# A mixture-of-experts loop: where the transposes, the rows given back and the down products stand in TensorE's list

## What is computed

```python
logits = t @ router_w + router_b
top_val, top_idx = lax.top_k(logits, 4)          # 4 of 32 experts for each token
gates = jax.nn.softmax(top_val, axis=-1)
...
# for each expert, with xe the rows of its tokens
gu = xe @ w_gu[e] + b_gu[e]                      # 1024 -> 2048
g, u = jnp.split(gu, 2, axis=-1)
g = jnp.minimum(g, 7.0)
u = jnp.clip(u, -7.0, 7.0)
act = (u + 1.0) * (g * jax.nn.sigmoid(1.702 * g))
y = act @ w_down[e] + b_down[e]                  # 1024 -> 1024
...
# weighted by the gates, added to the tokens' rows; then the gated residual add and rms_norm
```

## Time and profile before

| | |
|---|---|
| median of 3 runs | 1328.81 us |
| the profiled execution, own time | 1330.05 us |
| its span, first to last instruction | 1328.3 us |
| TensorE products, busy | 1272.8 us (96%) |
| TensorE weight loads, busy | 587.8 us (44%) |
| VectorE busy | 516.7 us (39%) |
| ScalarE busy | 178.1 us (13%) |
| read from memory | 476.10 MB, 359 GB/s over the span |

### The profile page before, as it was taken

The page is one execution under the profiler, slowest core; times in us unless marked ns, Lnnn a source line. Parts: engine busy times, 40 slices in busy tenths (PEclk is TensorE's granted clock), DMA queues, the critical chain, the costliest instruction groups (busy, mean ns, idle before and its releaser), DMA issues.

```text
span 1328.3 us, 16731 instructions
## 1 busy us (share of the span) xinstructions
PE 1272.8 (96%) x5975; PEld 587.8 (44%) x5976; DVE 516.7 (39%) x1144; ACT 178.1 (13%) x378; POOL 12.5 (1%) x31
## 2 busy tenths in 40 slices
PE   6999999999999999999999999999999999899997
PEld 4876866788753333333333333333333333233332
DVE  3022674331244434344343333333344344334344
ACT  2101322331021001000010000001100011001002
POOL 0000000110000000000000000000000000000000
PEclk8999999999999999999999999999999999999999
DMA  9857675326678999999999999999999999799995
GB/s 354 306 205 265 244 250 194 127 82 272 235 284 336 428 429 429 428 429 429 428 428 429 428 428 429 428 429 428 412 428 429 430 427 429 321 429 429 429 427 208
DMA packets 59182, 477.53 MB, mean 360 GB/s; under 512 B 4991, under 2 KB 5076, under 8 KB 32532
## 3 DMA queue, kind: packets, MB, share of 16 engines
q1 hardware_dynamic: 58852, 476.11, 87.3%
q10 hardware_dynamic: 304, 1.06, 0.2%
HBM read 476.10 MB, written 1.05 MB: 359 GB/s over the span
## 4 chain that ended last, share of the span: by engine, by line
PE 77%; DMA 18%; DVE 3%; issue 1%; ACT 1%; DVEq 0%; ACTq 0%; SPq 0%
PE bank L1610 24%; DMA down_ring<-in_w_down 17%; PE bank L1647 15%; PE bank L1294 11%; PE bank L1438 4%; PE bank L1287 4%; PE bank L1598 3%; PE bank L1576 3%; PE bank L1342 2%; PE bank L1501 2%; PE bank L1568 2%; DVE scratch L1125 1%; DVE scratch L1123 1%; DMA xres<-in_x 1%; PE bank L1677 1%
## 5 line engine op out<-in xcount | busy, mean ns | idle before, releaser
L1610 PE MATMUL bank<-gu_ring,scratch 128*64 128x512 f32 x2048 | 459.3, 595 | 1.6 <-DVE scratch L1055 1.6
L1610 PEld LDWEIGHTS bank<-gu_ring,scratch 128*64 128x64 f32 x2048 | 143.3, 137 | 284.7 <-issue 284.4
L1647 PE MATMUL bank<-down_ring,scratch 128*64 128x512 f32 x1024 | 235.5, 602 | 23.2 <-DMA down_ring<-in_w_down 18.1
L1294 PE MATMUL bank<-gu_ring 128*128 128x256 f32 x640 | 143.8, 381 | 0.0
L1647 PEld LDWEIGHTS bank<-down_ring,scratch 128*64 128x64 f32 x1024 | 71.0, 137 | 145.6 <-issue 133.5
L1294 PEld LDWEIGHTS bank<-gu_ring 128*128 128x128 f32 x640 | 119.8, 190 | 20.3 <-issue 4.0
L715 ACT ACTIVATE scratch<-bank 128x512 f32<-128x512 f32 x32 | 19.1, 597 | 684.6 <-PE bank L1610 684.6
L1113 DVE TENSOR_TENSOR scratch<-bank,bgu 128x512 f32<-128x512 f32 x32 | 22.1, 691 | 219.5 <-PE bank L1576 219.5
L1081 DVE TENSOR_TENSOR xres<-xres,bank 128x512 f32<-128x512 f32 x132 | 81.8, 681 | 58.5 <-PE bank L1598 58.5
L1576 PEld LDWEIGHTS bank<-ident,scratch 128*128 128x128 f32 x392 | 41.1, 140 | 79.5 <-ACT scratch L715 26.0
L1568 PE MATMUL bank<-xn,onehot 128*64 128x512 f32 x264 | 69.6, 605 | 0.0
(11 more groups left out here) (258 smaller groups left out, 797.9 us busy)
## 6 DMA issues: line engine op xcount, KB each, us to landing
gu_ring<-in_w_gu SPq DMA_DIRECT2D x128, 2048.0 KB, 23.5
down_ring<-in_w_down SPq DMA_DIRECT2D x64, 2048.0 KB, 17.3
gu_ring<-in_w_in SPq DMA_DIRECT2D x32, 1024.0 KB, 7.9
gu_ring<-in_w_ada SPq DMA_DIRECT2D x16, 1024.0 KB, 7.1
down_ring<-in_w_ada SPq DMA_DIRECT2D x8, 512.0 KB, 10.3
gu_ring<-in_w_ada SPq DMA_DIRECT2D x8, 512.0 KB, 11.4
gu_ring<-in_w_pa SPq DMA_DIRECT2D x4, 1024.0 KB, 6.3
gu_ring<-in_w_pb SPq DMA_DIRECT2D x4, 1024.0 KB, 6.2
```

The costliest lines, as they stand in the source:

```text
L1294: last = M(dst[:, b * T:(b + 1) * T], group_chunk(group, kt // 4)[:, kt % 4, cols], hT[:, kt, :], start=kt == 0, stop=kt == KT - 1)
L1610: last = M(bank[f // 2][64 * a:64 * a + 64, :], xT[:, kt % 4, kt // 4, :], gu_ring[:, 8 * half + kt, f * 512:(f + 1) * 512], start=kt == 0 ...
L1647: last = M(bank[7][64 * a:64 * a + 64, :], act_sb[:, kt % 4, kt // 4, :], down_ring[:, kt // 2, (kt % 2) * D + a * 512:(kt % 2) * D + (a + ...
```

## The change

- `give` moves from behind kt 1 of gate/up to the place behind all transposes, ahead of the further passes and the down products.
- Both halves of `take` of the next expert stand together ahead of the u transposes. Behind these come `way_back` and `take_transposed`, with no product between; the down products run without a break.
- `give` writes banks 0, 1, 2 and 4 in place of 4 to 7 (`GIVEN`).
- TensorE no longer waits for `given_added` ahead of `take`. It waits for it at the head of an expert, and in `further` ahead of its first products, there also for `xTe_ready` of the next expert.
- On VectorE `take` and then `add_given` stand directly behind the activation, ahead of the further passes. A memset of one column, behind a wait for the adds, raises `given_added` a fifth time for each expert, and one in front of the loop raises it once; ScalarE's last waits count with it.
- On ScalarE `copy_back` waits until `give` has read `back`, within the loop.

```diff
--- before.py
+++ after.py
@@ -367,6 +367,7 @@
             return 38 + n
 
         TURN_G2B = 42
+        GIVEN = (0, 1, 2, 4)
         EMPTIED_HT = KT
 
         block = ctx.enter_context(nc.Block())
@@ -694,6 +695,8 @@
             def copy_back(item):
 
                 act.wait_ge(back_done, item + 2)
+                if not isinstance(item, int):
+                    act.wait_ge(given_done, item * 4 + 4)
                 A(back[:], bank[5][:, 0:T], ACT.Copy).then_inc(back_ready, 1)
 
             def by_pairs(columns):
@@ -747,7 +750,7 @@
 
             for n in range(4):
                 tt, half = n // 2, slice(n % 2 * 512, (n % 2 + 1) * 512)
-                act.wait_ge(given_added, NE * 4 + n + 1)
+                act.wait_ge(given_added, NE * 5 + n + 2)
                 A(xn[:, 1, half] if tt else scratch[:, half], xres[:, tt, half], ACT.Square, accum_out=osq[:, n:n + 1]
                   ).then_inc(sq_done, 1)
                 if n == 2:
@@ -1067,6 +1070,7 @@
             V.tensor_scalar(passes[:, 2, :], passes_f[:, 1, :], 1.0, None, ALU.add)
             V.tensor_copy(passes[:, 0:2, :], passes_f[:]).then_inc(passes_ready, 1)
             take(0)
+            V.memset(small[:, 4:5], 0.0).then_inc(given_added, 1)
 
             dve.wait_ge(bdown_in, 32)
             dve.wait_ge(emptied, EMPTIED_HT + TURN_G2B + 1)
@@ -1078,7 +1082,7 @@
                     tt, half = n // 2, n % 2
                     cols = slice(half * 512, (half + 1) * 512)
                     dve.wait_ge(given_done, item * 4 + (n + 5))
-                    V.tensor_tensor(xres[:, tt, cols], xres[:, tt, cols], bank[4 + n][:, :], ALU.add
+                    V.tensor_tensor(xres[:, tt, cols], xres[:, tt, cols], bank[GIVEN[n]][:, :], ALU.add
                                     ).then_inc(given_added, 1)
 
             def further_pick(expert, first, made):
@@ -1104,7 +1108,6 @@
                             own.then(last)
                 last.then_inc(gated_ready, 1)
                 pick(item + 1)
-                add_given(item - 1)
                 count = further_count(dve, item)
                 before_it = dve.value_load(passes[0:1, 1, bass.ds(item, 1)], min_val=0, max_val=T * TOPK // FCAP)
                 further_pick(item, pass_start[:, 0:1], item + before_it)
@@ -1124,8 +1127,11 @@
                     own.then(V.tensor_scalar(u, u, LIMIT, -LIMIT, ALU.min, ALU.max))
                     V.scalar_tensor_tensor(act_sb[:, :, a, :], u, 1.0, sig[:, :, a, :], op0=ALU.add, op1=ALU.mult
                                            ).then_inc(act_ready, 1)
+                take(item + 1)
+                add_given(item - 1)
                 further_passes(dve, item, count, lambda b, k: further(item, b, k))
-                take(item + 1)
+                dve.wait_ge(given_added, item * 5 + 5)
+                V.memset(small[:, 4:5], 0.0).then_inc(given_added, 1)
 
                 dve.wait_ge(down_used, item * 2 + 2)
                 V.tensor_tensor(y_sb, bank[7][:, :], g2b, ALU.mult).then_inc(y_ready, 1)
@@ -1595,13 +1601,14 @@
                 for n in range(4):
                     tt, a = n // 2, n % 2
                     rows_ = slice(64 * a, 64 * a + 64)
-                    M(bank[4 + n][:, :], back[rows_, tt * P:(tt + 1) * P], y_sb[rows_, :], start=True, stop=True
+                    M(bank[GIVEN[n]][:, :], back[rows_, tt * P:(tt + 1) * P], y_sb[rows_, :], start=True, stop=True
                       ).then_inc(given_done, 1)
 
             def expert(item, half, fills):
 
                 count = further_count(pe, item)
                 pe.wait_ge(xTe_ready, item + 1)
+                pe.wait_ge(given_added, item * 5 + 1)
 
                 def gate_up(kt, parts):
 
@@ -1622,23 +1629,19 @@
                         gate_up(kt, range(4))
                     else:
                         gate_up(kt, (0, 1))
-                    if kt == 1:
-                        give(item - 1)
                 gate_up(KT - 3, (2, 3))
                 pe.wait_ge(raw_ready, item * 2 + 1)
                 transposes(2, g_raw).then_inc(gT_done, 1)
                 gate_up(KT - 2, (2, 3))
                 gate_up(KT - 1, (2, 3))
-                pe.wait_ge(given_added, item * 4 + 4)
-                take(item + 1, (0,))
+                take(item + 1)
                 pe.wait_ge(raw_ready, item * 2 + 2)
                 transposes(3, u_raw).then_inc(uT_done, 1)
-                take(item + 1, (1,))
                 way_back(item)
+                take_transposed(item + 1)
+                give(item - 1)
                 further_passes(pe, item, count, lambda b, k: further(item, half, fills, k))
                 for kt in range(KT):
-                    if kt == KT // 2:
-                        take_transposed(item + 1)
                     if kt % (KT // 2) == 0:
                         pe.wait_ge(act_ready, item * 2 + (1 + 2 * kt // KT))
                     if kt % 4 == 0:
@@ -1653,6 +1656,8 @@
             def further(expert, half, fills, k):
 
                 pe.wait_ge(xraw_ready, expert + 2)
+                pe.wait_ge(xTe_ready, expert + 2)
+                pe.wait_ge(given_added, expert * 5 + 5)
                 pe.wait_ge(f_onehot, (expert + k) * 2 + 2)
                 for tt in range(TT):
                     for q in range(4):
```

## The result

| | median of the runs (lowest to highest) | profiled execution | its span |
|---|---|---|---|
| before | 1328.4 (1326.42 to 1331.49), 7 runs | 1330.05 | 1328.3 |
| after | 1336.44 (1334.04 to 1339.43), 7 runs | 1337.38 | 1335.6 |

The ratio is 1.0058, with an interval of 1.0044 to 1.0072: 8.0 us slower by the medians, 7.3 by the two spans. The forecast of 1334.7 had the direction, and the range holds the median. The account behind it holds in most terms. Its largest miss is the clock, sized at 1.5 us where it cost about 5; the start of the stream was sized too small the other way.

The account below looks back on a forecast made before the run. The weight stream was taken to bound the kernel, with TensorE's lead nearly used up. Terms -0.7 -0.5 +5.7 -1.3 +1.2 gave +4.4, the clock's 1.5 made +5.9 on 1328.81: 1334.7 us, range 1330.7 to 1338.5.

Parts of the forecast that it names:

- the clock: In expert 25's further pass: one fall of TensorE's clock behind the new stand, +1.5 us, bounds 0 and 1.7.
- the start of the stream: At the first experts: loads for expert 2 released 2 us earlier without `give` in front, -0.7 us, bounds -0.1 and -1.5.
- The bound: In the expert loop: the weight stream limits; TensorE's lead over it is 0.7 us at expert 25, 1.5 at 31.
- The steady expert: An undisturbed expert on TensorE takes 0.85 us less, 26.5 instead of 27.38, bounds 0.3 and 1.0.
- The prices of the excursions: Breaks from TensorE's 64-column products for transposes: fixed price 0.30 us each, plus 0.11 per transpose.
- Expert 25: Kt 6 starts 0.5 us earlier; then the pass's first products wait for the adds, +5.7, bounds +2.0 and +6.3.
- To the end: Behind the issue of 26's down weights: stream without a gap, then expert 31's lead -1.3 us and tail +1.2.
- The lead at 31: Expert 31's kt 6 products start nearer behind the landing of their weights, -1.3 us.
- The tail: Rest of expert 31 behind its kt 6 start, now with `give` in it: excursions 4.15 against 3.0, +1.2 us.
- the third rival: Two or three clock falls on the path, each adding up to 1.7 us: 1336 to 1338; chance 0.25.
- the issue of 26's down weights: Sign at the end of expert 25: this load issued near 1153 or 1154 us instead of 1148.97.
- the stretch without transfer: Sign in the weight stream around expert 25's pass: its second gap without transfer is 4 us longer.

Follow-up runs that it names:

- a_pad: The changed kernel with one more product of 512 columns ahead of `give` in every expert; 1334.77 us, 1.0027 of the kernel before.
- b_fill: The kernel before with products without a use in two stands of its further pass (one and two products); 1327.91 us, 0.9983.
- b_give: The kernel before with only `give` moved, behind `way_back` and ahead of the pass, `take` left in halves; 1332.84 us, 1.0027.
- b_merge: The kernel before with only the transposes put together and the down products unbroken, `give` staying behind kt 1; 1330.44 us, 1.0017.
- a_perbank: The changed kernel with the pass released bank by bank, bank 4 written first and added ahead of `take`; 1330.69 us, 1.0000 of the kernel before.
- a_again: The changed kernel run once more with no edit, as base for three other kernels; 1336.24 us, 1.0054 of the kernel before.
- a_fill: The changed kernel with products without a use in all three stands of the pass (four, one and two); 1331.26 us, 1.0012 of the kernel before.
- a_busy: The changed kernel with four products without a use in front of the pass's wait for the adds; 1336.1 us, 1.0031 of the kernel before.
- b_pass4: The kernel before with five products of 512 columns at the head of the further pass, starting it later; 1332.85 us, 1.0018.

## Why the prediction was right, and where it was not

**The bound.** Right in what it said. The reading that the lead of TensorE over the stream was 0.7 us at expert 25 and 1.5 at 31, so that a faster expert had nowhere to put its gain, is what the pair without the pass shows (13.9 us less work, no less time), and a_pad from the other side. The 0.7 itself is one execution's: in b_fill, whose list is the same up to there, TensorE waits 0.75 us for those weights.

**The steady expert.** -0.85 forecast, -0.90 measured (27.38 to 26.48). The way there was incomplete. The prices of the excursions bear up: less their new waits of 0.33 and 0.80 us, b_give and b_merge take 27.04 and 26.70. What I did not price is which waits such a saving lays bare; in the full change `give` happens to cover the activation, and there the sum was lucky.

**The start of the stream.** -0.7 forecast, -1.35 between the profiled executions, but that is not this term. The first gate/up product of the loop stands at 400.28 in the trace of before and at 398.71 in that after, 1.57 apart; over all fourteen traces it stands between 395.9 and 400.3, by scatter of the phases ahead of the loop. Counted from that product, the landing of 25's last gate/up weights comes 714.1 to 715.9 us later in the five traces with `give` behind kt 1, mean 714.9, and 712.3 to 714.3 in the nine with `give` behind the transposes, mean 713.2. The loads for expert 2 are released 2.0 us earlier in these, as foreseen. The term is some -1.7, beyond the bound of -1.5.

**Expert 25.** Right: -0.69 for -0.5, and +5.53 for +5.7, with the stand of 3.75 us that I worked out as 3.7 from VectorE's list. a_perbank takes most of the stand away and, within its interval, the loss with it.

**To the end.** The lead at 31 was -1.43 for -1.3. The tail is +2.93 for +1.2; in a_again, with no fall of the clock there, it is 1333.03 - 1304.67 = 28.36, +1.22 on the 27.14 of before. Not foreseen was that from the issue of 26's down weights to the landing of 31's last gate/up weights, 30 loads, it takes 149.72 us instead of 150.73. The change does that. Those down weights are two loads, each issued when half of 25's down products are done. Unbroken down products release the second 3.4 us behind the first, with transposes in the middle it is 4.2, and the queue is empty just then: the second lands 4.89 behind the first instead of 5.87. In the eight traces with the pass and unbroken down products the whole stretch is 149.5 to 149.8, in the four with broken ones 150.4 to 151.4, and what follows the second load's landing is 137.0 to 137.1 in all twelve. So this term is -1.0, and I had it at nothing.

**The clock: the step that failed.** "I expect one such fall, in the pass, where nothing hides it [...] I take 1.5, bounds 0 and 1.7." In the profiled execution it was 3.35 in the pass and 1.7 behind expert 31's weights, together 5.1; by the medians of a_again and a_fill those in the pass alone cost 5.0. What was right is the mechanism, a fall behind the new stand. Two things were off. The fall behind the long stand lasted 10.2 us and not 3.4, in both profiled executions of the changed kernel. And the waits of 2.1 us for weights, and the wait of 2.6 within the pass, which had left the clock alone in the one trace that I had the earlier trace rows, are followed by falls in some executions. What came is thus the third rival, several falls on the path, to which I gave 0.25; I held against it that one of nine bound experts before was followed by a fall, which was a count of waits that nothing depended on, from one execution. That the forecast was only 1.7 us below the median is luck in part, two errors that work against each other: the clock cost 3.5 us more than I took, and the other terms come to +1.9 (-1.7 -0.7 +5.5 -1.0 -1.4 +1.2) and not to +4.4. Together these make an estimate of 6.9, for 8.0 measured; a_fill less b_fill gives 3.35 where the terms without the clock give 1.9. Of the signs that I named, the issue of 26's down weights came at 1155.81 and not near 1153 or 1154, and the stretch without transfer is 7.9 us longer and not 4, mostly by the 3.35 of clock ahead of that issue.

**Transposes in a row.** In a_fill ten transposes stand in a row in every expert, and its granted clock is 1.00 from 1105 to 1150. In all fourteen traces every fall between 406 and 1312 us stands at a wait of TensorE of 1.9 us or more, and none at transposes. The rule of the Trainium skill ("TensorE: Matmul & The Clock Gate", Part 4, the PE-mode transpose) that transposes do not count as work of TensorE in the same way is not seen to matter in these runs, and I was right to leave it out of the sum.

## What to carry to other kernels

Before an engine's list is shortened, look at how far ahead of it its data lands at the places where it must wait last; a lead of 0.7 us is all that a saving can reach, whatever the engine's busy share says. Where a change puts waits for several results in front of rare work that nothing hides, release it by the one result that it needs first: here that gave back the loss within the interval. A stand of TensorE on the critical path is to be priced with what the clock does behind it, from more than one execution; products without a use in such a stand kept the clock up, and cost nothing where they ended before the wait did.

## What the runs showed of the hardware

- **A fall of TensorE's clock behind one stand can last 10.2 us.** Behind the stand of 3.75 us the granted clock stayed at 0.50 (1.2 GHz) that long in both profiled executions of the changed kernel, while TensorE went through the pass's first products and into its gate/up products (24 of their 64 records). Behind the stand of 2.88 in a_pad it lasted 6.8, from 1127.4; on the paths behind waits shorter than that, 3.4 each.
- **The same wait is followed by a fall in one execution and not in another.** Behind the wait of 2.6 us within the pass there is none in the kernel before and none in the first run of the changed one (32 products in 3.64 us), but one in a_again, a_busy, a_perbank, a_pad, b_give, b_merge and b_pass4 (5.33 to 5.34). The three kernels that had shortened it to 0.8 had none.
- **Products without a use in the stands keep the clock**, at no cost where they end before the wait does: 0.42% of this kernel (1.0054 to 1.0012).
- **What a late second load loses on an empty queue is not made up.** With the second 2 MB load issued 3.4 us behind the first they landed 4.88 to 4.90 us apart in eight traces; issued 4.2 behind, 5.42 to 6.78 apart in four. The 28 loads behind them took 137.0 to 137.1 in all twelve, so nothing made up for it.
